# Six row buffers in place of eight in the gather stage of a two-block kernel

## What is computed

```python
q = jnp.einsum('td,dhk->thk', xc, w_query)           # 8 heads, 2 sides of 128
s = jnp.einsum('thpk,hpnk->thpn', q, sub_keys)       # 128 scores a side
top_s, top_i = lax.top_k(s, PEER_TOPK)               # 16 of each side
best_s, best_pos = lax.top_k(cand_s, PEER_TOPK)      # 16 of the 256 sums
g = jax.nn.softmax(best_s, axis=-1)
u = jnp.take(expert_u, idx, axis=0)
v = jnp.take(expert_v, idx, axis=0)
act = jax.nn.gelu(jnp.einsum('td,thkd->thk', xc, u))
y = jnp.einsum('thk,thkd->td', (g * act).astype(v.dtype), v)
```

## Time and profile before

| what | value |
| --- | --- |
| median of 3 runs | 1332.79 us |
| the profiled execution | 1332.18 us |
| its span in the profile | 1330.4 us |
| PE, DVE, ACT, POOL busy | 86%, 73%, 43%, 43% of the span |
| DMA, mean over the span | 281 GB/s |
| DMA, slices 22 to 39 of 40 | 408 to 428 GB/s |
| chain that ended last | PE 41%, DMA 27%, DVE 20% |

### The profile page before, as it was taken

The page is one execution under the profiler, slowest core; times in us unless marked ns, Lnnn a source line. Parts: engine busy times, 40 slices in busy tenths (PEclk is TensorE's granted clock), DMA queues, the critical chain, the costliest instruction groups (busy, mean ns, idle before and its releaser), DMA issues.

```text
span 1330.4 us, 15786 instructions
## 1 busy us (share of the span) xinstructions
PE 1146.2 (86%) x5672; PEld 797.6 (60%) x5672; DVE 970.6 (73%) x1944; ACT 570.7 (43%) x1031; POOL 576.7 (43%) x576
## 2 busy tenths in 40 slices
PE   6999899999999998967868888698887787778787
PEld 6988797999999978855753443244432222223222
DVE  5589999973777665654688877777777777777554
ACT  5477677654435445883433322333332223222221
POOL 0199999999920000000024444344444444444331
PEclk9999999999999998988889999999999999999999
DMA  7545343444554554321569999999999999999996
GB/s 262 191 132 183 125 133 127 144 142 159 182 198 160 187 187 156 128 73 60 169 268 423 427 426 428 426 427 427 426 426 425 419 422 423 425 418 408 426 427 261
DMA packets 128671, 374.37 MB, mean 281 GB/s; under 512 B 6864, under 2 KB 84688, under 8 KB 95696
## 3 DMA queue, kind: packets, MB, share of 16 engines
q0 software_dynamic: 36864, 268.45, 48.1%
q1 hardware_dynamic: 89376, 100.15, 23.0%
q10 hardware_dynamic: 2352, 4.77, 1.1%
HBM read 372.29 MB, written 1.05 MB: 281 GB/s over the span
## 4 chain that ended last, share of the span: by engine, by line
PE 41%; DMA 27%; DVE 20%; issue 6%; ACT 6%; ACTq 0%; POOL 0%; SPq 0%; DVEq 0%; POOLq 0%
DMA row<-in_experts,big 16%; PE unit L402 10%; DMA big<-in_experts,big 10%; PE unit L403 10%; PE unit L404 10%; PE unit L635 6%; DVE w_lo L1216 3%; DVE work L1578 3%; DVE conv_acc L1239 1%; DVE big L1502 1%; ACT probs L983 1%; DVE big L1511 1%; DVE big L1508 1%; DVE conv_acc L1505 1%; DVE big L1590 1%
## 5 line engine op out<-in xcount | busy, mean ns | idle before, releaser
L402 PE MATMUL unit<-in_hi,w_hi 128*128 128x256 f32 x1216 | 376.0, 309 | 7.7 <-DVE probs L1450 4.8
L403 PE MATMUL unit<-in_lo,w_hi 128*128 128x256 f32 x1216 | 345.9, 284 | 0.0
L404 PE MATMUL unit<-in_hi,w_lo 128*128 128x256 f32 x1216 | 345.7, 284 | 0.0
L1908 POOL DMA_INDIRECT row<-in_experts,big x128 | 125.8, 983 | 478.0 <-DVE big L1571 303.4
L635 PE MATMUL unit<-row,probs 128*128 128x512 f32 x512 | 250.6, 616 | 53.8 <-ACT probs L983 52.7
L983 ACT ACTIVATE probs<-ident,big 128x128 f32<-128x128 f32 x256 | 102.8, 402 | 450.7 <-DVE big L1590 450.7
L1216 DVE TENSOR_TENSOR w_lo<-w_raw,w_hi 128x2048 fp32r<-128x2048 f32 x91 | 211.8, 2329 | 98.2 <-ACT w_hi L738 98.2
L402 PEld LDWEIGHTS unit<-in_hi,w_hi 128*128 128x128 f32 x1216 | 235.3, 194 | 26.1 <-issue 22.0
L403 PEld LDWEIGHTS unit<-in_lo,w_hi 128*128 128x128 f32 x1216 | 235.5, 194 | 16.2 <-issue 16.0
L635 PE MATMUL unit<-big,probs 128*128 128x512 f32 x384 | 187.6, 623 | 61.1 <-ACT probs L983 61.0
L404 PEld LDWEIGHTS unit<-in_hi,w_lo 128*128 128x128 f32 x1216 | 235.1, 193 | 0.0
(11 more groups left out here) (246 smaller groups left out, 1313.0 us busy)
## 6 DMA issues: line engine op xcount, KB each, us to landing
w_raw<-in_w_in SPq DMA_DIRECT2D x58, 1024.0 KB, 5.2
w_raw<-in_w_mem_kv SPq DMA_DIRECT2D x8, 1024.0 KB, 5.2
w_raw<-in_w_out SPq DMA_DIRECT2D x8, 1024.0 KB, 5.1
w_raw<-in_w_query SPq DMA_DIRECT2D x6, 1024.0 KB, 5.5
w_raw<-in_w_diff_proj SPq DMA_DIRECT2D x4, 1024.0 KB, 5.1
w_raw<-in_w_x_proj SPq DMA_DIRECT2D x4, 1024.0 KB, 5.2
w_raw<-in_w_conv_proj SPq DMA_DIRECT2D x4, 1024.0 KB, 5.1
row<-in_experts,big POOLq DMA_INDIRECT x128
```

The costliest lines, as they stand in the source:

```text
L402: e.matmul(unit[:, to], *hi_hi, start=first, stop=False)
L403: e.matmul(unit[:, to], *hi_lo, start=False, stop=False)
L404: m = e.matmul(unit[:, to], *lo_hi, start=False, stop=final)
L1908: e.indirect_dma_start(out=UV.ap(g), out_offset=None, in_=experts, in_offset=bass.IndirectOffsetOnAxis(ap=expert[t][:, n:n + 1], axis=0)). ...
```

## The change

The third split pair `w2` is made in the lasting space, so it is not given back. All pieces go round in three pairs to the end. `early_space` then holds `in1` alone and gives back 16 KB of a partition, in which two row buffers lie, and not four. The list of row buffers has six entries: the two on `in1`'s memory, `big[2]`, `big[0]`, `big[1]` and `conv_in`. In the list before these are the first six, in this order. The two that are dropped are those on `w2`'s memory, which waited for the last piece of pq1.

```diff
@@ -169,8 +169,8 @@
 
         split = [split_pair(ctx, f"w{i}", PIECE) for i in range(2)]
         lasting_pair = split_pair(ctx, "in0", T)
+        split = Ring("split", split + [split_pair(ctx, "w2", PIECE)])
         early_space = ctx.enter_context(ExitStack())
-        split = Ring("split", split + [split_pair(early_space, "w2", PIECE)])
         early_pair = split_pair(early_space, "in1", T)
         units = Ring("unit", [psum(f"unit{i}", 1024) for i in range(3)])
         banks = Ring("bank", [psum(f"bank{i}", 512) for i in range(2)])
@@ -337,13 +337,11 @@
         load_order = [*range(FIRST_UNDER + 2), FIRST_UNDER + 4, FIRST_UNDER + 5,
                       FIRST_UNDER + 2, FIRST_UNDER + 3]
         for p in range(PIECES_ALL):
-            split.take(p, None if p < FIRST_UNDER + 2 else (p - FIRST_UNDER) % 2)
+            split.take(p)
         early_space.close()
-        rows = [sb(f"row{i}", [2 * D])[:, :] for i in range(4)]
-        rows = [*rows[2:], big[2][:, :], big[0][:, :], big[1][:, :],
-                flat(conv_in[:, :, :])[:, 0:2 * D], *rows[:2]]
-        ROW_FREE = ([("pair free", "mix")] * 2 + [("x2", 1)] * 3 + [("h3", 1)]
-                    + [("piece", FIRST_UNDER + 1)] * 2)
+        rows = [*(sb(f"row{i}", [2 * D])[:, :] for i in range(2)), big[2][:, :], big[0][:, :],
+                big[1][:, :], flat(conv_in[:, :, :])[:, 0:2 * D]]
+        ROW_FREE = [("pair free", "mix")] * 2 + [("x2", 1)] * 3 + [("h3", 1)]
         UV = Ring("uv", rows)
         diag_places = [probs.buffers[i % 2][:, i // 2 % 2, i // 4 * P:(i // 4 + 1) * P]
                        for i in range(12)]
```

## The result

The changed kernel takes 1370.29 us, the median of 4 runs (1365.47 to 1378.21), against 1332.15 of the kernel before in 4 runs on the same chip (1329.72 to 1333.75). The ratio is 1.0289, 95% interval 1.0259 to 1.0319: **38.1 us more**. The forecast was 1337.1 with a range to 1345.0. The direction was right and the size was off by a factor of nine. The profiled execution is the slowest of the four, 1378.21 us with a span of 1376.5; its stage of the experts, from the first gather to the last dot product, takes 691.1 us where it took 643.9, that is 47.3 more. The lines of this kernel are two lower: gather L1906, dot product L1576, weighing L1588, diagonal L981, the experts' matmul L633.

What follows compares the result with a forecast made beforehand. The stream of expert rows by DMA was taken as the bound. Losses of 3.0, 1.0 and 0.3 us at three places sum to 4.3, added to the median of 1332.79: 1337.1 us, range 1333.5 to 1345.

Steps and rivals of the forecast that it cites:

- (b): Row-buffer ring: two gathers fewer at the start, later ones wait for the row six before, not eight; whole 4.3 us.
- (c): Third split pair stays, so pq3's pieces go to pairs 2 and 0 and casts wait for earlier pieces: nothing.
- (d): Waits of the two dropped rows for the last piece of pq1 go, already met when the gathers came: nothing.
- Costs nothing as long as it starts 5.2 us or more before the dot product of row g+6: Rule for the gather that row g sets free, 5.2 us from start to landing; only three places fail it.
- The 13.04 us: Steady stretch before the change, gather to its dot product; 8.1 with six buffers against 5.2 needed, 2.9 to spare.
- The start: First rows of the experts: DVE's late releases no longer hidden, dot product 17 late by 2.9; taken as 3.0 us.
- The release of row 69: Start of the second quarter, ACT casting a weight piece: gather for row 75 lands late, 1.0 us in the sum.
- The release of row 202: Row whose matmuls ran at the lower granted clock: its gather, starting at 1198.53, lands 0.3 us late.
- Latency above 5.8: Rival: margin runs out in ordinary cycles, gaps at casts and table loads; about 8.8 us, 1341.6, tail to 1350; chance 0.20.
- Latency about 4.4: Rival: gathers land sooner, only the start loses much; 2.2 to 2.4 us, 1335.1; chance 0.15.
- The laggards catch up: Rival: late DMA engines at the stage's end run faster, up to 6 us back, 1331.1; chance 0.10.
- Each dot product 2.45 after the one before: Profile sign for the steady stretch: spacing stays 2.45 us; more would mean a latency above 8.

Runs made afterwards that it cites:

- six_old_split: Kernel before with only the row-buffer ring cut to six, third split pair still given back: 1373.32 us, ratio 1.0327.
- six_weigh_first: Changed kernel with the weighing of row g put ahead of the dot product of row g+1, six buffers kept: 1337.35 us, ratio 1.004.
- gathers_one: Experts' dot products, weighing, diagonals and matmuls left out; each gather waits only for the landing of the one before, one under way: 2173.51 us.
- the pure streams: Gathers without the experts' work, at most two, three or four under way: 1456.05, 1355.86, 1319.77 us; three and four timed again: 1346.16, 1321.33.
- six_no_gelu: Changed kernel with the experts' Gelu replaced by a copy, so ACT has no table to bring back: 1359.0 us, ratio 1.0196.
- eight_no_gelu: Kernel before, eight buffers, with the experts' Gelu replaced by a copy: 1331.52 us, ratio 1.0002.
- five_rows: Kernel before with the ring cut to five row buffers: 1468.01 us, ratio 1.1014.
- three_halves: Gathers without the experts' work, three rows under way, each row filled by two half-size gathers with their own semaphores: 1415.46 us, ratio 1.0617.

## Why the prediction was wrong, step by step

**That all is in (b), the ring: right.** six_old_split, which leaves out (c), loses the same. The dropped waits (d) are gone in it too, but also in six_weigh_first, which costs 5.3 us.

**"Costs nothing as long as it starts 5.2 us or more before the dot product of row g+6": this step failed.** It turned the latency of a lone gather into a threshold, with no cost above it. The latency itself was right: 5.5 us in the median of gathers_one against 5.2 taken. But a row is there only when the last engine has brought its part, and that last part does not come as in a lone gather. Gathers 10 and 11 of the changed kernel took 8.1 and 8.5 us with only one or two ahead of them, and the pure streams show that throughput falls already at three under way, where the threshold leaves some 1.5 us to spare. The number that the step needed was the rows under way, and the throughput at that number. The sum had both halves of it at hand: the time from gather to dot product, 8.1 us, is 3.3 rows at 2.45. It was read as a margin of 2.9 us over a latency. It should have been read as 3.3 rows under way, for which the steady stretch of the trace of before, with about 5.3 under way, showed no throughput at all.

The 13.04 us were also those of the last engine alone. In 900 to 1300 of the kernel before, the middle one of a gather's sixteen updates came 8.1 us after its start and the last 13.0 (medians over the gathers). So most engines had not 7.8 us above the 5.2 but 2.9, less than the 4.9 of two rows. In the changed kernel the two are 7.2 and 8.6: the shorter ring holds the engines closer together. What that costs by itself no run shows.

The Trainium skill, "DMA: Bandwidth & Descriptors", section on the anatomy of one DMA, has the same form, a fixed 2.0 us plus the bytes at full rate, 4.4 us here. The lone gathers take 5.3 to 5.9 in that window, so it is low, and used as a threshold it would have gone further astray. The same page's section on latency and other measured facts says that the latency of HBM is 0.2 us on average and 2 us at high load. That points to the side on which the runs fell; no run here shows it apart from the rest.

**The size of the three terms.** The start: forecast 3.0, measured 7.3 here (4.8 and 5.1 in the other two kernels of six that use the full work, six_old_split and six_weigh_first). The release of row 69: forecast 1.0; between rows 74 and 75 4.23 us pass (884.77 to 889.00) in place of 2.14 (869.18 to 871.32), so 2.1. The release of row 202: forecast 0.3; 3.58 us between rows 207 and 208 in place of 2.44, so 1.1. Each of the three places was sized low, together 10.5 us of the 47.3 in the profiled execution. The places of the last two were rightly named, but they are two of 19 rows with a step of 1.0 us or more, and the measure found none of the other 17.

**The term that was missing**, the other 37 us of that execution, was put at nothing because of the threshold. The runs part the whole loss in another way. Of the 38.1 us between the medians the table loads on ACT make 11 (six_no_gelu against the change, while eight_no_gelu shows them hidden at eight), and 27 stay, the start included, of the same size as the 24.8 by which the pure stream falls from four to three. That the 27 are this loss and nothing else is an inference from the size. Counted up to the last semaphore update, the changed kernel has three rows under way for 63% of the time between 900 and 1300, four for 29% and two for 7%. And the mean number does not give the throughput by itself: six_no_gelu, with 3.5 by the count used above, moves 404 GB/s where the pure stream moves 409 at three (inside what three vary by), and five_rows, with 2.6, moves 343 where the pure stream moves 356 at two. Uneven releases are a likely reason; how much of the 27 us is theirs stays open.

**What the forecast describes well is another kernel.** six_weigh_first has 4.1 rows under way, and there its picture holds: 5.1 us lost at the start, 2.0 up to row 75, 0.9 up to row 208, nothing in the ordinary cycles, 5.3 us in the timed runs. The picture of a stream with a few gaps is true where the gaps stand in a full stream.

**The rivals.** *Latency above 5.8* was the right side: gaps in many cycles with table loads, as its text says, a cost that rises steeply. At 8.8 us with a tail to 1350 it was far too small, because it had the same form. The forecast's own sum gives 22 us at 6.7; to reach 38 it would need more still, which only one of the 256 lone gathers took (7.5). *Latency about 4.4*: refuted by gathers_one. *The laggards catch up*: half of it came true. In 1364 to 1368 DMA is busy 0.71, so most engines end near 1366.8, and the last dot product waits for its data until 1368.3; the spread is 1.5 us where it was some 6. By the sixteen updates of the last gather, fourteen engines of the kernel before ended between 1316.0 and 1316.6 and two at 1319.0 and 1322.3. No kernel here with the whole work was faster for the smaller spread.

**What the changed profile was to show.** Six gathers 1.2 to 1.5 apart and then none for ten us: yes (677.23 to 683.65, then 694.19). A DMA share below 1 between 696 and 715: 0.91, yes. The chain's DMA pieces at 8.1 in place of 13: 6.8 to 10.0, yes. Fewer GB/s in the slice around 866: 372, with 389 and 418 beside it, yes. Dot product 17 at 730.2: 733.26, with a first gather 1.2 us earlier than before, so no. Each dot product 2.45 after the one before: no, 2.67 in the mean from row 17 on ((1368.34 - 733.26) / 238), and that was the sign that the forecast itself had named for a latency above 8; the median time from gather to dot product is 8.8 from row 20 on.

## What to carry to other kernels

When buffers are taken away from a stream that is the bound, don't compare the time that is left with the latency of a lone transfer: divide it by the period to get the transfers under way, and ask at what number the throughput was ever measured. If the trace has only one number, the price is unknown, and the range must say so. The kernel with fewer transfers and nothing else is quickly made and gives the curve. Where the trace holds the end of each engine's part, read when most of them end, not only when the last does.

The time for which a buffer is held counts like a buffer: here 2.1 us less of it were worth nearly one of 2.45, 33 us with six buffers and nothing with eight. And a late release that costs nothing in a deep ring (the table loads with eight buffers) costs time in a short one (11 us with six), so its price must be taken at the new depth. None of these kernels with the whole work is measurably faster than the one before; if six buffers must do, weighing first gives 1337.35 us.

## What the runs showed of the hardware that was not expected

*A DMA share near 1 is not a full stream.* With two, three and four gathers under way the share is 0.97, 1.00 and 1.01, and the stream moves 356, 409 and 427 GB/s. Some packets of 8 KB are longer instead: the mean is 384, 358, 324 and 310 ns with one, two, three and four under way, 327 in the changed kernel and 311 before, while the median is 309 in all six. So GB/s must be read beside the share, against the best value of the same kernel.

*A short queue makes the time vary.* Ten runs of three gathers under way span 27 us (1337.94 to 1364.8), four runs of four 2.2 us, the four of the changed kernel 12.7, those of the kernel before 4.0. The profiled execution of the change happened to be its slowest, 7.9 us above the median, so its terms add to 47 and not to 38.

*An indirect gather costs POOL as much for half a row as for a row*: 0.94 us and 0.30 of issue in three_halves as in the changed kernel. At two gathers a row POOL's issuing, 2.5 us, becomes as long as the transfer.
